# Three-branch attention: VectorE takes an item's row maximum ahead of its copy of turned rows

## The reference, cut to what matters

```python
def masked_softmax(s, mask):
    s = jnp.where(mask, s.astype(jnp.float32), -jnp.inf)
    m = jnp.max(s, axis=-1, keepdims=True)
    ...
    e = jnp.where(mask, jnp.exp(s - m), 0.0)
    return e / jnp.maximum(jnp.sum(e, axis=-1, keepdims=True), 1e-30)

# nsa_mixer, for a block of 128 queries
s_c = jnp.einsum('bqghd,bngd->bghqn', qb, kc) * scale
p_c = masked_softmax(s_c, cmp_end[None, :] <= t[:, None])
o_c = jnp.einsum('bghqn,bngd->bqghd', p_c.astype(vc.dtype), vc)
...
p_s = masked_softmax(s_s, valid_s[:, :, None]).astype(v_g.dtype)
o_s = jnp.einsum('bghqk,bgqkd->bqghd', p_s, v_g)
...
p_w = masked_softmax(s_w, valid_w).astype(vw.dtype)
o_w = jnp.einsum('bghqk,bkgd->bqghd', p_w, vw)
out = gb[..., 0:1] * o_c + gb[..., 1:2] * o_s + gb[..., 2:3] * o_w
```

## Time and profile before

| | us |
|---|---|
| median of 3 runs (lowest, highest) | 1934.3 (1933.65, 1935.55) |
| the profiled execution, its own time | 1934.45 |
| its span, first to last instruction | 1932.7 |
| around the span | 1.75 |
| PE busy over the span | 1845.4 (95%) |
| DVE, ACT, POOL busy | 1022.2, 827.7, 588.2 (53%, 43%, 30%) |
| the attention stage that the change touches | about 1374 to 1542 of the span |
| mean granted TensorE clock | 0.989 of full |

### The profile page before, as it was taken

The page is one execution under the profiler, slowest core; times in us unless marked ns, Lnnn a source line. Parts: engine busy times, 40 slices in busy tenths (PEclk is TensorE's granted clock), DMA queues, the critical chain, the costliest instruction groups (busy, mean ns, idle before and its releaser), DMA issues.

```text
span 1932.7 us, 27356 instructions
## 1 busy us (share of the span) xinstructions
PE 1845.4 (95%) x10538; PEld 1446.1 (75%) x10538; DVE 1022.2 (53%) x2005; ACT 827.7 (43%) x1566; POOL 588.2 (30%) x419
## 2 busy tenths in 40 slices
PE   8999999997878999999999999999899999999998
PEld 7878889832223777767888888899777778888886
DVE  3271452521112859663476767723577625767677
ACT  4223641311111542475545444352476646454543
POOL 3343431011110323365321132242155543132111
PEclk9999999998999999999999999999999999999999
DMA  7233303799999312211222233311203012233321
GB/s 240 92 107 111 131 1 153 275 397 420 420 419 371 116 44 88 88 45 45 79 96 87 88 126 112 135 47 45 44 2 88 2 44 88 88 118 111 120 87 44
DMA packets 86866, 252.04 MB, mean 130 GB/s; under 512 B 12212, under 2 KB 19700, under 8 KB 74448
## 3 DMA queue, kind: packets, MB, share of 16 engines
q1 hardware_dynamic: 81344, 238.79, 33.6%
q0 software_dynamic: 4592, 9.30, 1.3%
q10 hardware_dynamic: 800, 2.20, 0.3%
HBM read 241.89 MB, written 15.73 MB: 133 GB/s over the span
## 4 chain that ended last, share of the span: by engine, by line
PE 85%; DVE 5%; DMA 3%; issue 3%; ACT 3%; POOL 0%; ACTq 0%; DVEq 0%; POOLq 0%
PE psA L1599 41%; PE psS L2047 5%; PE psA L1642 3%; PE psA L2011 3%; PE psO L1829 2%; PE psT L1829 2%; PE psS L1829 2%; PE psO L2349 2%; PE psT L2399 2%; DMA ring<-in_w_down_e 2%; DVE x L3076 1%; DMA big<-in_w_down_e 1%; PE psA L1464 1%; PE psA L1778 1%; PE psS L1642 1%
## 5 line engine op out<-in xcount | busy, mean ns | idle before, releaser
L1288 POOL TENSOR_TENSOR w_slot<-ring,w_slot 128x1024 fp32r<-128x1024 f32 (+1 forms) x81 | 214.1, 2658 | 523.1 <-ACT w_slot L2428 522.9
L1599 PE MATMUL psA<-hT_hi,w_slot 128*128 128x512 f32 x960 | 297.8, 389 | 0.0
L2428 ACT ACTIVATE w_slot<-ring 128x1024 fp32r<-128x1024 f32 (+2 forms) x183 | 196.8, 1086 | 163.2 <-DVE ring L3076 75.0
L1599 PEld LDWEIGHTS psA<-hT_hi,w_slot 128*128 128x128 f32 x960 | 180.2, 188 | 37.4
L1599 PE MATMUL psA<-hT_lo,w_slot 128*128 128x512 f32 x480 | 186.7, 389 | 0.0
L3076 DVE TENSOR_TENSOR w_slot<-ring,w_slot 128x1024 fp32r<-128x1024 f32 x98 | 119.9, 1225 | 116.0 <-ACT w_slot L2428 116.0
L3076 DVE TENSOR_TENSOR x<-psA,x 128x512 f32<-128x512 f32 (+1 forms) x186 | 117.1, 662 | 104.2 <-PE psA L1599 68.8
L1599 PE MATMUL psA<-w_slot,hid_part 128*128 128x512 f32 x672 | 161.4, 389 | 0.0
L2428 ACT ACTIVATE big<-psA 128x512 f32<-128x512 f32 (+5 forms) x135 | 62.3, 483 | 210.3 <-PE psA L1599 121.2
L2428 ACT ACTIVATE scr<-scr,stat 128x384 f32<-128x384 f32 (+3 forms) x224 | 124.2, 555 | 53.6 <-DVE stat L4068 44.0
L1599 PEld LDWEIGHTS psA<-w_slot,hid_part 128*128 128x128 f32 x672 | 126.1, 188 | 26.2
(11 more groups left out here) (542 smaller groups left out, 4418.3 us busy)
## 6 DMA issues: line engine op xcount, KB each, us to landing
ring<-in_mlp_w SPq DMA_DIRECT2D x32, 2048.0 KB, 8.2
ring<-in_w_in SPq DMA_DIRECT2D x8, 2048.0 KB, 8.2
ring<-in_w_gate_e SPq DMA_DIRECT2D x14, 1024.0 KB, 16.7
ring<-in_w_up_e SPq DMA_DIRECT2D x14, 1024.0 KB, 21.5
ring<-in_w_down_e SPq DMA_DIRECT2D x13, 1024.0 KB, 27.5
big<-in_w_down_e SPq DMA_DIRECT2D x12, 1024.0 KB, 27.8
ring<-in_ab_w_in SPq DMA_DIRECT2D x5, 2048.0 KB, 8.5
scr<-in_w_down_e SPq DMA_DIRECT2D x7, 1024.0 KB, 26.6
```

What stands on the lines that cost most here:

```text
L1288: nc.gpsimd.tensor_tensor(part(w_lo, c), raw_piece(c), part(w_hi, c).bitcast(F32), ALU.subtract)\
L1599: ins = pe.matmul(o, a, b, start=(at == 1), stop=(at == 3 * len(terms)))
L2428: return nc.scalar.activation(o, i, f, **kw)
```

## The change

In DVE's loop for this attention, the copy of the turned rows (of item i - 6, at odd steps) stood ahead of the row maximum of item i. Now it stands behind it, and still ahead of the reciprocal. Nothing else is changed: the same instructions, the same waits, the same buffers.

```diff
                     elif i - 2 in NSA_STEPS and NSA_JOBS[NSA_STEPS.index(i - 2)][0] == "query":
                         queries(NSA_JOBS[NSA_STEPS.index(i - 2)][1])
-                    k = i - TURN_LAG - 1
-                    if 0 <= k < n_nsa and k % 2:
-                        dve.wait_ge(n_turned, k + 1)
-                        if k >= TURNED:
-                            dve.wait_ge(n_values, values_before(k - TURNED))
-                        nc.vector.tensor_copy(turned_probs[k % TURNED][:, 0:nsa[k]["n"]], psT[k % 2][:, 0:nsa[k]["n"]])\
-                            .then_inc(n_copied[k % 2], 1)
                     if i < n_nsa:
                         it = nsa[i]
                         dve.wait_ge(n_scores, i + 1)
...
                                 op0=ALU.add, op1=ALU.min, accum_out=negm[:, n_items + i:n_items + i + 1]).then_inc(n_masked, 1)
+                    k = i - TURN_LAG - 1
+                    if 0 <= k < n_nsa and k % 2:
+                        dve.wait_ge(n_turned, k + 1)
+                        if k >= TURNED:
+                            dve.wait_ge(n_values, values_before(k - TURNED))
+                        nc.vector.tensor_copy(turned_probs[k % TURNED][:, 0:nsa[k]["n"]], psT[k % 2][:, 0:nsa[k]["n"]])\
+                            .then_inc(n_copied[k % 2], 1)
                     if 2 <= i < n_nsa + 2 and nsa[i - 2]["g"]:
                         weigh_nsa(i - 2)
```

## The result

The changed kernel takes 1921.09 us (median of 4 runs, 1920.52 to 1922.27), beside 1934.01 us of the kernel before in the same comparison (4 runs, 1933.65 to 1935.55). The ratio is 0.9932, with a 95% interval of 0.992 to 0.9944: faster by 12.9 us.

What follows compares the result with a forecast made beforehand. PE was held by waits for ACT's copies, late through DVE's row maxima; 8.6 + 0.5 + 0.59 + 0.53 = 10.2 us off 1934.45 gave 1924.3 us, range for 8 in 10 1922.4 to 1928.6.

Steps and rivals of the forecast that it cites:

- all 15 waits: PE's waits ahead of its transposes for ACT's copy in this attention stage, 8.6 us in sum, forecast to go.
- POOL's one: The one wait of PE's transposes put down to POOL, 0.5 us, forecast to go with the earlier reciprocal.
- its cover: DVE's wait for PE ahead of its copies, 45.6 us over 38 copies, said to hide the row maximum's 0.61 us.
- The reciprocal's step: DVE's reciprocal comes 0.61 us earlier, right behind the copy, so POOL's product is no longer 0.27 us late for PE.
- the rival on POOL: Without the earlier reciprocal PE waits for POOL, 0.27 us 15 times; 4.1 us stay, time 1928.4 us; chance 0.14.
- The waits for queries: PE's wait of 1.86 us ahead of the queries' transposes at step 9, and gaps ahead of it, were to stay.
- the stretch of half clock: PE at 1.2 GHz from 1389.4 to 1392.8, priced at 1.7 us, expected again; chance of a different clock 0.06.
- The two small waits of the earlier trace: First steps: scores of items 17 and 16 wait 0.59 us for a row maximum and 0.53 for ACT; both go.
- the second rival: By the page's rule the two psT banks are short, so nothing is gained and time stays 1934.3 us; chance 0.05.
- the sum of 10.2 us: Total gain forecast for the stage from the removed waits, equal to PE's idle time counted by windows from 1400 on.
- longer transposes: A transpose group behind a wait lasts 0.63 in place of 0.60 us, 16 of them, 0.5 us more gained; let cancel.
- The rival on a slower kernel: DVE's copy becomes the late one, 0.35 us at each of 64 pair-item copies, time 1946.6 us; chance 0.04.

Runs made afterwards that it cites:

- e5: The changed kernel with DVE's copy moved behind the reciprocal too (row maximum, reciprocal, copy): 1921.77 us.
- e3: The changed kernel with the reciprocals that stand behind a copy put behind the next step's row maximum, as late as before the change: 1924.5 us.
- e7: The changed kernel with the copy put ahead of the reciprocal in the attention of the layer before as well: 1924.3 us.
- e2: The changed kernel with the new order only at steps 27 to 43, 61 to 77, 95 to 111 and the last, the old order elsewhere: 1931.69 us.
- e9: The kernel of e6 with the reciprocal of pair items ahead of the copy from step 112 on: 1917.78 us.
- e4: The changed kernel with every fourth group of PE's transposes, from item 8 on, also waiting for the latest DVE copy: 1932.31 us.
- e6: The changed kernel with ACT and DVE taking out the last four head pairs' queries one step earlier: 1917.37 us.

## Why the prediction was right, and where it was wrong

*What was right.* The chain from DVE's late row maximum over ACT's exp and copy to PE is what held PE. With the row maximum 2.54 us earlier, all 15 waits and POOL's one went. The copy cost nothing in its new place (no wait of PE for it), and e5 shows that its cover is larger than needed, except behind cmp items. The reciprocal's step was needed: e3 lost 3.4 us without it, where the rival on POOL had 4.1. The waits for queries and the stretch of half clock came again as said: in the changed kernel it is this window, 1.2 GHz in place of 2.4:

```profile
1390.50:1393.90 3.40, 3.40 (x17) 3.40 (x17) 2.27 (x9) 2.38 (x8) 0.88 (x2) 0.52 0.00 0
```

Behind the stage nothing was given back: from its end to the end of the span it is 390.9 us before and 390.8 after. The two small waits of the earlier trace rows went from 0.53 + 0.59 to one of 0.16. The rule of the Trainium skill on gaps that repeat (Perfetto Trace Analysis, Identifying Performance Opportunities), the second rival, does not hold for the trace here (the page says only that such a gap can mean this): the same two psT banks serve a stage without those gaps, 13.3 us shorter. These 15 gaps were ones of order alone. The four waits of the layer before, where PE waits for a copy that starts as early as it can (e7), may be of the page's kind; no run adds a bank.

*What was wrong* is the size of one term, the sum of 10.2 us: "8.6 + 0.5 + 0.59 + 0.53 = 10.2 us, the same as the idle time counted by the windows", and with it the sentence that no reordering can take more out of this part. The stage gave 13.3 us. The agreement of waits and windows was no check, since both count the same printed gaps. A gap in PE's rows begins at the modelled end of the row before, while in an unbroken flow the next group starts ahead of that end. The place of the earlier trace rows shows it. Before, the scores ahead of the wait start at this row, and the transposes at 1485.74:

```profile
1483.81 0.62 PE L2386 MATMUL psS<-nsa_k,nsa_q 128*128 128x384 f32 x2
```

That is 1.93 us from start to start. In the changed kernel it is 1478.85 - 1478.42 = 0.43 us. The gain is 1.50 us where 1.32 was printed as idle; 0.16 of the 0.18 between them is overlap (1478.42 + 0.59 - 1478.85) and the rest the longer scores row. By batches, 2.3 us more than printed came at the 16 places, 0.5 at the waits of the earlier trace rows and 0.5 in batches in which PE showed no wait; less the 0.16 us of wait that stayed this is the missing 3.1. I had seen only the smallest piece of it, 0.03 us a group for longer transposes, and let it cancel.

The trace of before held a warning in a row that I passed over. The waits of the weight loads for the same groups:

```profile
PEld psT L2399 <- POOL scr L1436: 12.2, 16, 1.6
PE psT L2399 <- ACT big L2428: 8.6, 15, 1.3
...
PE psT L2399 <- POOL scr L1436: 0.5, 1, 0.5
```

12.2 us in 16 waits, beside 9.1 in 16 for the matmuls. Three of these are short ones at other places, and three of PE's stand under "issue" among the weight loads; taken place by place from the timeline, the weight loads show 13.2 us for PE's 16. (They name POOL, whose count is the earlier of the two that the instruction waits for.) What these places were worth, 11.4 us, lies between the two: the matmuls' rows show too little and the weight loads' too much. With 0.18 us added to each of PE's 16 waits the sum would have been 10.2 + 2.9 = 13.1 us and the time 1934.45 - 13.1 = 1921.4, 0.3 from the median. That is hindsight and in part luck: the 0.18 is known from the changed kernel's trace alone, and the 16 places differ, from -0.14 to 0.32.

Four smaller things were wrong and didn't move the sum. "The pattern comes back every four items in every second block and is absent in the others" misses two of the 15 waits, 0.16 and 0.30 us, inside the second block. The stretch of half clock was priced at 1.7 us, half of its length; e2's stage, without it, is 1.16 us shorter in that part. The rival on a slower kernel took the waits of the earlier trace rows as those of a copy that comes late behind row maximum and reciprocal; that copy starts when PE's transposes let it, after 0.71 to 1.22 us of idle DVE. And the busy times in the second window are 26 to 36 us, not 24 to 36.

*Open.* The 0.52 us of e9, the losses of e5 and the 1.16 us for the clock come from one profiled execution each. Why e2 has no stretch at half clock isn't known. Nor is it why the price beyond the idle time is there in most places and absent at four narrow ones of e4. Whether the reciprocal ahead of the copy gains in the other narrow blocks wasn't tried.

## What to carry to other kernels

When two engines take turns, put first on each the step that starts the longer chain, and leave the one that waits anyway for last; then look at what else moved with it (here a reciprocal, worth 3.4 us). Price a wait from start to start against the same group in a part that flows, not by the idle time printed; here the worth lay between the idle time of the matmuls (9.1 us) and that of the weight loads (13.2 us), and the weight loads show waits that the matmuls' rows hide. An order that is right in one loop is not a rule for its neighbour: in the layer before, the copy put ahead of the reciprocal cost 3.2 us, as the reciprocal had stood in idle time. And look at who is idle ahead of the instruction that is waited for, before calling it late.

## What the runs showed of the hardware that was not expected

- Groups of transposes behind scores start 0.16 us before the modelled end of the scores' row in an unbroken flow, at 128x384 (1478.85) and at 128x128 (1513.06) alike. Two batches of e6 were 0.25 us longer than the same ones of e9 (3.36 and 3.32 us, and 3.11 and 3.07), with no idle time printed on PE in either.
- The stretch of 3.4 us at half clock (1.2 GHz) follows the gaps of 1.63 and 1.86 us on PE in seven of the eight traces that have these gaps. In e2 the same gaps leave the granted clock at 1.00 (2.4 GHz) through the whole window, as do gaps of 0.91, 0.90 and 0.41 us in their place in e6.
- A stretch of 3.4 us at half clock cost 1.16 us of stage (22.56 us with it, 21.40 in e2), not half of its length.
